# Product-key expert layer with 48 instead of 42 tokens of the last tile done by gathers

## The reference

```
q = (xb @ w_query).reshape(TOKEN_BLOCK, PEER_HEADS, 2, PEER_QDIM // 2)
s = einsum("nhpd,hpkd->nhpk", q, sub_keys)          # 8 heads, 2 x 128 keys
sv, si = top_k(s, 16); the 16 x 16 sums of the two halves; top_k of these, 16
eidx = first index * 128 + second index              # 8 x 16 = 128 experts per token
g = softmax(top_s)                                   # 128 gates per token
u = u_tab[eidx]
hid = gelu(einsum("nd,ned->ne", xb, u), approximate=False)
w = g * hid
return einsum("ne,ned->nd", w, v_tab[eidx])          # v_tab: 16384 x 2048, like u_tab
```

## Time and profile before

| | |
|---|---|
| median of 3 runs | 3321.6 us (3310.88, 3321.6, 3322.99) |
| profiled execution | 3307.15 us, its span 3305.2 us |
| PE busy | 3226.5 us, 98% of the span |
| DVE busy | 2707.6 us, 82% |
| POOL, ACT busy | 1158.6 us (35%), 1055.8 us (32%) |
| bytes moved by DMA | 914.54 MB, mean 277 GB/s |

### The profile page before, as it was taken

How to read it: one execution, slowest core, us unless ns; L and a number is a source line. 1 busy time by engine, 2 the same in 40 slices (tenths; PEclk the granted TensorE clock), 3 DMA queues, 4 the chain that set the end, 5 groups by cost and what they waited for, 6 DMA issues and landing times.

```text
span 3305.2 us, 48430 instructions
## 1 busy us (share of the span) xinstructions
PE 3226.5 (98%) x19393; PEld 2975.4 (90%) x19393; DVE 2707.6 (82%) x3839; ACT 1055.8 (32%) x1398; POOL 1158.6 (35%) x592
## 2 busy tenths in 40 slices
PE   5999999998999999999999999999999999999998
PEld 2788888888995448999999999999999999999997
DVE  2599999999785669969888888888688888888888
ACT  3322323233222004952323322333332333332332
POOL 2433333332541765013333333333133333333331
PEclk8999999999999999999999999999999999999999
DMA  9744544445547112569999999989799998999896
GB/s 385 287 168 158 174 162 166 168 166 209 208 169 301 64 39 89 234 254 365 353 359 359 352 361 360 355 347 371 288 368 354 359 347 351 355 352 354 349 341 269
DMA packets 174475, 914.54 MB, mean 277 GB/s; under 512 B 16303, under 2 KB 54104, under 8 KB 80088
## 3 DMA queue, kind: packets, MB, share of 16 engines
q1 hardware_dynamic: 125046, 553.37, 45.3%
q0 software_dynamic: 49248, 358.63, 27.6%
HBM read 876.31 MB, written 34.55 MB: 276 GB/s over the span
## 4 chain that ended last, share of the span: by engine, by line
PE 86%; DVE 7%; DMA 3%; POOL 2%; issue 1%; ACT 1%; SPq 0%; DVEq 0%; POOLq 0%; ACTq 0%
PE ps_all L1041 17%; PE ps_all L1108 9%; PE ps_all L1102 9%; PE ps_all L1103 9%; PE ps_all L1048 9%; PE ps_all L727 7%; PE ps_all L729 7%; PE ps_all L728 7%; PE ps_all L1006 6%; DVE sb_hot L2018 2%; DMA sb_small<-in_ada_w 2%; DVE sb_hot L2015 1%; DMA sb_raw_ring<-in_v_t 1%; PE ps_all L706 1%; DVE sb_raw_lo L1934 1%
## 5 line engine op out<-in xcount | busy, mean ns | idle before, releaser
L1433 ACT ACTIVATE sb_raw_hi<-sb_raw_ring 128x2048 fp32r<-128x2048 f32 x256 | 491.0, 1918 | 1136.6 <-DMA sb_raw_ring<-in_v_t 540.5
L1934 DVE TENSOR_TENSOR sb_raw_lo<-sb_raw_ring,sb_raw_hi 128x2048 fp32r<-128x2048 f32 x256 | 585.3, 2286 | 107.0 <-ACT sb_raw_hi L1433 106.9
L1041 PE MATMUL ps_all<-sb_h_hi,sb_raw_hi 128*128 128x342 f32 x2048 | 646.1, 320 | 0.5 <-ACT sb_gelu_sb L1440 0.5
L1041 PE MATMUL ps_all<-sb_h_lo,sb_raw_hi 128*128 128x342 f32 x2048 | 645.7, 320 | 0.0
L1102 PE MATMUL ps_all<-sb_w_hi,sb_raw_hi 128*128 128x342 f32 x2032 | 640.0, 320 | 4.9 <-DVE sb_w_lo L2039 2.9
L1103 PE MATMUL ps_all<-sb_w_lo,sb_raw_hi 128*128 128x342 f32 x2032 | 639.3, 320 | 0.0
L2267 POOL DMA_INDIRECT sb_gather_ring<-in_u_tab,sb_kept x171 | 295.1, 1726 | 744.1 <-DVE sb_kept L2064 561.9
L2267 POOL DMA_INDIRECT sb_gather_ring<-in_v_tab,sb_kept x171 | 301.0, 1760 | 623.5 <-DVE sb_acc_a L2077 412.0
L2172 POOL TENSOR_TENSOR sb_w_low<-sb_w_raw,sb_w_high 128x1536 fp32r<-128x1536 f32 (+1 forms) x63 | 261.6, 4153 | 403.5 <-ACT sb_w_high L1243 403.5
L1102 PEld LDWEIGHTS ps_all<-sb_w_hi,sb_raw_hi 128*128 128x128 f32 x2032 | 385.4, 190 | 7.0 <-issue 3.6
L1041 PEld LDWEIGHTS ps_all<-sb_h_hi,sb_raw_hi 128*128 128x128 f32 x2048 | 385.4, 188 | 0.7 <-ACT sb_raw_hi L1433 0.7
(11 more groups left out here) (309 smaller groups left out, 5378.9 us busy)
## 6 DMA issues: line engine op xcount, KB each, us to landing
sb_raw_ring<-in_u_t SPq DMA_DIRECT2D x128, 1024.0 KB, 6.9
sb_raw_ring<-in_v_t SPq DMA_DIRECT2D x128, 1024.0 KB, 7.5
sb_arena<-in_ada_wt SPq DMA_DIRECT2D x96, 512.0 KB, 4.3
sb_w_raw<-in_w_t SPq DMA_DIRECT2D x32, 1024.0 KB, 5.8
sb_small<-in_ada_w SPq DMA_DIRECT2D x31, 1024.0 KB, 13.2
sb_w_raw<-in_w_v SPq DMA_DIRECT2D x32, 768.0 KB, 4.3
sb_g_ring<-table_scratch SPq DMA_DIRECT2D x32, 684.0 KB, 9.8
table_scratch<-sb_stage SPq DMA_DIRECT2D x8, 2432.0 KB, 8.2
```

The source lines that it names most:

```text
L1041: last = mm(acc, raw_hi[:, r[0], kk * P:(kk + 1) * P], part[:, kk, :], start=i == 0, stop=False)
L1433: acti(raw_hi[:, k % 2, :], raw_ring[:, k % RAW, :], ACT.Copy).then_inc(S["un_hi"], 1)
L1934: vec.tensor_tensor(raw_lo[:, k % RAW, :], raw_ring[:, k % RAW, :], raw_hi[:, k % 2, :].bitcast(f32), ALU.subtract)\
```

## The change

`XT` goes from 42 to 48 and `STAGE` from 38 to 42. What follows from it:

| | before | after |
|---|---|---|
| dense tokens `ND`, columns of each expert matmul | 342 | 336 |
| stages of the gate table, tokens in each | 9 x 38 | 8 x 42 |
| groups in the table stretch (`NGROUP`), full and of two tokens | 90: 81 and 9 | 88: 80 and 8 |
| groups of the last tile's tokens `XG`, partitions in use | 3 x 42 = 126 | 2 x 48 = 96 |
| slots of a group `XSLOTS` | 43 | 64 |
| gathers per table `DOTS` | 171 | 192 |
| bytes of one `g_ring` load | 684 KB | 672 KB |
| dots: units with one and with two, of 116 | 61 and 55 | 40 and 76 |
| multiply-adds: units with one and with two, of 118 | 65 and 53 | 44 and 74 |

`slot_at` places one extra gather in three now, and the stage buffers and the start of one SBUF region are placed anew.

```diff
-XT = 42
+XT = 48
 XG = P // XT
 XP = XG * XT
@@
-STAGE = 38
+STAGE = 42
@@
 def slot_at(n):
-    m, j = n // 4, n % 4
-    return (False, SLOTS + m) if j == 1 else (True, 3 * m + max(j - 1, 0))
+    m, j = n // 3, n % 3
+    return (False, SLOTS + m) if j == 1 else (True, 2 * m + j // 2)
@@
         hid_all = take(DOTS)
+        at = max(at, SM + 2 * PEER_HEADS * NKEYS)
@@
-        stage = [placed(f"stage{n}", a, [P, NKEYS, STAGE]) for n, a in enumerate((M0, at))]
+        stage = [placed(f"stage{n}", a, [P, NKEYS, STAGE]) for n, a in enumerate((M0, at) if NSTAGE % 2 else (at, M0))]
```

## The result

The changed kernel is slower: 3450.8 us in the median of its runs (3426.3 to 3476.2), against 3316.4 for the kernel before (3310.9 to 3323.0), a ratio of 1.041 [1.038, 1.045], or +134 us. The forecast was 3348 us with a range up to 3393: its sign was right, its size was not. The profiled execution took 3476.17 us, 169 more than the one shown of before, so the traces have somewhat more to explain than the medians.

The account below looks back on a forecast made before the run. The prediction took PE as today's bound and the DMA engines, at share 0.97, as the next: +20 us up part, +12 down part, -4.5 small parts, together +27 on 3321.6, giving 3348 us, range 3292 to 3393.

Parts of the forecast that it names:

- DVE and the gather ring: Expert units: VectorE's list plus waiting for gathers into freed buffers costs 7.36 us a up-part unit, 7.44 in the down part.
- Each further us of landing adds 0.33 us a unit.: Up-part units: later gather landing delays VectorE once in three units; about 10 us of landing gives 7.7 us a unit.
- By this count the DMA engines become the bound.: Expert units: DMA load of 7.49 us (up) and 7.42 (down) exceeds PE's 7.39; at share 0.97, 7.72 and 7.65.
- the forecast's own range: Whole kernel, DMA share near 0.97: 3325 to 3372 us, chance 0.45.
- PE at 96 to 98: Stretches of 100 us between 1600 and 3200 us: PE busy 96 to 98 of 100 us instead of 100.
- Matmul pitch: Undisturbed expert units: matmuls of 336 columns every 153.3 to 154.7 ns, 154.0 taken, against 157.2 before.
- Bytes: Gather queue q0: 42 more gathers, 44 MB more, so q0 moves 402.7 MB.
- Rows 11: VectorE's waits: for gathers up from 3.8 us to some tens of us, for the gelu down from 148.0.
- Table stretch: Table stretch, where PE waits for DVE: one full and one half group fewer save 2.2 us.
- The first, PE as the bound: Rival, all expert units: PE stays the bound, DMA engines carry 388 GB/s, landing stays 9.0 us; 3281 us, chance 0.12.
- the third: Rival, expert units: DMA rate stays at 363 GB/s, units take 7.91 and 7.83 us; 3393 us, chance 0.21.
- the listed signs of being wrong: Units of 7.4 us, pitch still 157, DMA share under 0.94 with long gather waits, rate under 365 GB/s, longer table stretch.

Follow-up runs that it names:

- the dense list of before: The kernel before, with its 171 dots and multiply-adds placed as densely as in the changed kernel, same work and bytes: 3345.4 us, 1.009 [1.007, 1.010].

## Why the prediction was wrong

- **The failing step** is in "DVE and the gather ring": 0.28 us until the gather is issued and 9.0 us until it lands, "in all 9.3", of which only the landing was expected to grow, to "about 10 us", through busier DMA engines. GpSimd was taken as always free to start, and the length of its instruction, which the 9.0 us have in them, as fixed. The earlier trace rows held 2.74 and 0.94 us for the same work, and the mean of 1.73 us said that the long kind was common; the prediction gives no reason for either. By the semaphores' times in the traces, the way from a freed buffer to the landed gather took 9.6 us in the mean before, and after it took 12.0 in the up part (up to 19.8) and 11.0 in the down part. Of the 2.4 us more in the up part, 1.1 pass before the instruction starts, because GpSimd is held in an earlier one, 1.1 in the instruction itself, and 0.25 behind it. With the blocks taken away by waits alone, 112 of the 134 us go.
- **"Each further us of landing adds 0.33 us a unit."** The ring's rule was right in kind: by it 12.0 us would give 7.36 + 0.33 x 2.7 = 8.25 us a unit, measured were 8.68, and the dense list of before lost 30 us without long blocks. What was wrong is what goes into it. That the median landing came out at 10.0 us, as forecast, is luck: counted from the end of the instruction it was 7.5 us before and 7.4 after in the up part, so the rise is GpSimd's and not the DMA engines'.
- **"By this count the DMA engines become the bound."** Not in the changed kernel, whose share fell to 0.86 and 0.91. Where the blocks are gone or mostly gone (the up parts of the two kernels with one-input dots) it comes back: 7.58 and 7.59 us a unit at 0.97 and 0.98, 380 GB/s. The forecast had 7.72 at 0.97, because a unit's load was counted 1 to 2% too high. 3339 to 3341 us with the waits is inside the forecast's own range, with units of 7.81 and 7.60 us at a share of 0.95 (the run with a wait in each unit). That the engines are what bounds any of these runs is read from the shares, not isolated.
- **The clock.** No term stood for it. PE at 96 to 98 was forecast in small gaps. It had nine of over 5 us in the units from 17 on, up to 10.4, and behind eight of them the matmuls started at the lower level: at most 44 us.
- **Matmul pitch**: right within its bounds. The 100 us from 1700 on have 641 matmuls in 98.6 us, 153.8 ns. **Bytes**: q0 moved 402.68 MB, as said. **Rows 11**: waits for gathers up and the wait for the gelu down, as said, but 180.6 us and not some tens. **Table stretch**: PE starts unit 17 at 1469.6 us in place of 1473.8, 4 us sooner, 2 expected.
- **The rivals**: none described this. The first, PE as the bound, did not come true; the third had a rate stuck at 363 GB/s, and 380 over 800 us refutes it. It is also above the 358 GB/s that the prediction cites from the Trainium skill, on a core that runs alone. One of the listed signs of being wrong came true: a DMA share under 0.94 with long waits for gathers.
- **The Trainium skill** had the rule that was missed. "SBUF — State Buffer", section "Who interferes with whom", has VectorE and GpSimd lock a shared pair of ports for a whole instruction, and VectorE takes it also with two SBUF inputs, against a GpSimd operation that reads SBUF. The trace agrees in kind: held gathers end 0.81 us after the end of a VectorE instruction. It goes further than the Trainium skill in that 66 were held over 3.2 us, one for 11.05 us through eight instructions. And the Trainium skill infers that such a two-input operation leaves descriptor generation alone. For these gathers the runs show the opposite (2.77 us with two inputs, 1.52 with one, 0.99 with one and a wait). They read their indices from SBUF, which may be the difference; a plain DMA from GpSimd was not tried, and the one-input sums lack a write as well.

Open: why one boundary between two VectorE instructions lets a gather through and another doesn't; which part of the change brings the long blocks, since the dense list with the columns and units of before has none; and what is left between 3327 to 3341 us and the 3281 of a kernel that PE alone bounds. No version was measurably faster than the kernel before.

## What to carry to other kernels

A GpSimd gather's own duration in the trace is a measure of contention: if the same gather takes 0.94 us at one place and 2.7 or 11 at another, see what VectorE runs beside it, and count the late issue in the ring's round trip. VectorE instructions with two SBUF inputs back to back can hold a gather through several of them, and busy share does not tell whether they will (621 of 800 us with 66 such gathers, 694 with two); one short stand, placed where a buffer comes free, can give back far more than it costs (112 us here, nothing in the kernel before, which had only one long block). Before more work is put on an engine that is only third by busy share, ask which other engine lives from its gaps.

## What the runs showed of the hardware

- GpSimd's indirect gather is held by VectorE's two-input fp32 instructions in SBUF, and ends 0.81 us after the end of one of them. Mostly that is the one beside it (2.7 to 3.0 us in all), also where the next follows at once; in 66 of 384 cases of the changed kernel the gather took over 3.2 us, up to 11.3. What decides it is open; with a wait of DVE for the gather's issue (0.10 us in the case shown) none of 384 took over 3.1.
- The 16 DMA engines of a core that ran alone moved 380 GB/s over 800 us with matmuls running.
- A gather into 96 partitions took more engine time than one into 128: an estimated 3.0 to 3.3 us against 2.67.
- In the case shown, a gap of 10.41 us in PE's work was followed by matmuls 0.28 us apart (granted clock at the lower level, 1.2 GHz); from 1692.03 on, at the upper level, they stand 0.15 apart.
